# Half of the rounds' modulation columns as weighted rows on VectorE, in a fused fp32 two-block network

## The reference, cut to what matters

```python
c_act = jax.nn.silu(c)                       # (1, 1024)
for layer in range(DEPTH):
    mod = c_act @ mod_w[layer] + mod_b[layer]            # 6 x 1024 columns
    sh1, sc1, g1, sh2, sc2, g2 = jnp.split(mod, N_MOD, axis=-1)
    u = modulate(rms_norm(h, norm_mix[layer]), sh1, sc1)
    mix = hgrn2_mixer(u, ...)                            # layer 0
    h = h + g1[:, None, :] * mix
    u = modulate(rms_norm(h, norm_ffn[layer]), sh2, sc2)
    h = h + g2[:, None, :] * swiglu(u, ffn_w_in[layer], ffn_w_out[layer])
```

## Time and profile before

| | us |
|---|---|
| median of 3 runs | 1589.38 |
| their range | 1589.01 to 1591.5 |
| the profiled execution's own time | 1587.78 |
| its span in the profile | 1585.7 |

### The profile page before, as it was taken

One profiled execution on the slowest core, in us unless ns is written; L12 is line 12 of the kernel. 1 busy time (PEld: TensorE's weight loads), 2 busy tenths in 40 slices (PEclk: granted clock), 3 DMA queues, 4 the chain that ended last, 5 costly groups with the idle time before them and its releaser, 6 DMA issues.

```text
span 1585.7 us, 26563 instructions
## 1 busy us (share of the span) xinstructions
PE 1505.1 (95%) x11356; PEld 1247.4 (79%) x11356; DVE 743.4 (47%) x1185; ACT 581.7 (37%) x899; POOL 28.0 (2%) x47
## 2 busy tenths in 40 slices
PE   7999998999998979999999899989899999999996
PEld 4988898999998649999999768979666656566553
DVE  4658667677767335545555635644221212222121
ACT  3522243444444445444446625542121222212121
POOL 0100000000000001000000000001000000000000
PEclk9999999999989799999999779999999999999998
DMA  9778447978868404555534313716599999999995
GB/s 365 248 237 286 143 135 282 328 269 298 298 222 298 130 1 142 197 186 184 181 114 133 129 37 101 292 54 240 229 418 424 422 420 424 422 420 425 420 420 222
DMA packets 168467, 404.15 MB, mean 255 GB/s; under 512 B 5013, under 2 KB 131250, under 8 KB 155058
## 3 DMA queue, kind: packets, MB, share of 16 engines
q1 hardware_dynamic: 166336, 397.43, 67.4%
q0 software_dynamic: 1648, 5.18, 1.1%
q10 hardware_dynamic: 386, 0.11, 0.0%
HBM read 401.63 MB, written 1.07 MB: 254 GB/s over the span
## 4 chain that ended last, share of the span: by engine, by line
PE 79%; DMA 10%; DVE 7%; ACT 3%; issue 1%; SPq 1%; DVEq 0%; ACTq 0%
PE ps L1797 27%; PE ps L2332 11%; PE ps L2045 7%; PE ps L2354 5%; DMA arena<-in_w 4%; PE ps L1832 4%; PE ps L1810 3%; PE ps L2319 3%; DMA late<-in_w 2%; PE ps L2077 2%; PE ps L1977 2%; PE ps L1906 2%; PE ps L1896 2%; PE ps L2365 1%; DMA arena<-in_mod_w 1%
## 5 line engine op out<-in xcount | busy, mean ns | idle before, releaser
L1797 PE MATMUL ps<-u,wsplit 128*128 128x256 f32 x3912 | 485.9, 285 | 8.5 <-DVE wsplit L1147 6.9
L1797 PEld LDWEIGHTS ps<-u,wsplit 128*128 128x128 f32 x3912 | 477.0, 193 | 16.5 <-DVE wsplit L1147 8.7
L1147 DVE TENSOR_TENSOR wsplit<-arena,wsplit 128x1024 fp32r<-128x1024 f32 x258 | 312.1, 1222 | 255.6 <-ACT wsplit L759 253.9
L759 ACT ACTIVATE wsplit<-arena 128x1024 fp32r<-128x1024 f32 x258 | 270.7, 1056 | 334.2 <-PE ps L1797 161.5
L2332 PE MATMUL ps<-arena 128*64 128x256 f32 x1408 | 156.9, 380 | 4.8 <-DMA arena<-in_w 4.0
L2332 PEld LDWEIGHTS ps<-arena 128*64 128x64 f32 x1408 | 101.2, 137 | 65.9 <-issue 13.6
L2045 PE MATMUL ps<-hid,wsplit 128*128 128x256 f32 x1056 | 130.2, 283 | 0.3 <-DVE hid L1387 0.3
L2045 PEld LDWEIGHTS ps<-hid,wsplit 128*128 128x128 f32 x1056 | 128.2, 192 | 0.5 <-DVE hid L1387 0.5
L1703 DVE TENSOR_TENSOR arena<-arena,ps 128x256 f32<-128x256 f32 x32 | 13.5, 422 | 244.0 <-ACT arena L1106 244.0
L1111 ACT ACTIVATE arena<-ps 64x512 f32<-64x512 f32 x64 | 37.9, 592 | 145.3 <-PE ps L2354 144.5
L1832 PE MATMUL ps<-wsplit,u 128*128 128x256 f32 x672 | 84.9, 288 | 0.0
(11 more groups left out here) (352 smaller groups left out, 1441.1 us busy)
## 6 DMA issues: line engine op xcount, KB each, us to landing
arena<-in_w SPq DMA_DIRECT2D x66, 2048.0 KB, 25.1
late<-in_w SPq DMA_DIRECT2D x30, 2048.0 KB, 25.6
arena<-in_mod_w SPq DMA_DIRECT2D x48, 1024.0 KB, 6.5
arena<-in_ffn_w_in SPq DMA_DIRECT2D x44, 1024.0 KB, 5.3
arena<-in_ffn_w_out SPq DMA_DIRECT2D x22, 1024.0 KB, 5.0
arena<-in_a_w_in SPq DMA_DIRECT2D x16, 1024.0 KB, 8.6
arena<-in_kv_mod_w SPq DMA_DIRECT2D x8, 1024.0 KB, 4.9
arena<-in_kv_w SPq DMA_DIRECT2D x8, 1024.0 KB, 8.2
```

The source lines that it names most:

```text
L759: act.activation(piece_buf(p, 0), piece_src(p), ACT.Copy).then_inc(hi_done, 1)
L1147: dve.tensor_tensor(piece_buf(p, 1), piece_src(p), piece_buf(p, 0).bitcast(F32), ALU.subtract).then_inc(lo_done, 1)
L1797: mm = pe.matmul(o, w_[:, k, :], u[:, x_, k, :], start=first, stop=last)
```

## The change

The 4096 columns 2048 to 6144 of the first modulation matrix are divided. The first 2048 of them (g1, sh2) now go as weighted rows on VectorE: eight new slots of 128 x 2048 weights. The other 2048 (sc2, g2) stay `gemv`, one slot to a round in place of two. The eight rows slots stand in the ring behind the gate and query pairs 2 to 7 (six of them) and behind the value pairs of rounds 0 and 1. VectorE adds the first six up behind gate pieces 3, 5 and 7 and query pieces 1, 3 and 5, and the last two behind `products(1)` and `products(2)`, in the passes r = 0 and r = 1. `row_sums` stands behind the products of round 3, ScalarE copies its result behind the copy of value pair 3, and `columns` stands ahead of round 4's products, where `column(0)` stood. The sum takes the place of the output gates' buffer, which is written only later.

```diff
@@ rows_slot, plan()
-        s = slot("rows", "modkv" if n == 0 else "mod1", 2048 * max(n - 1, 0))
+        s = slot("rows", *(("mod0", 2048), ("modkv", 0), ("mod1", 0), ("mod1", 2048), ("mod1", 4096))[n])
...
-    linear("zf", "a_in", D + 256, 3, "act")
-    linear("q", "a_in", 0, 4, "act")
+    jobs["rows_a"] = []
+    for i in range(1, 8):
+        job, first = (("zf", D), ("q", -D))[i // 4]
+        linear(job, "a_in", first + 256 * i, 1, "act")
+        if i > 1:
+            jobs["rows_a"].append(rows_slot())
     for r in range(8):
         part, first = ("v", 2 * D) if r < 4 else ("g", 3 * D)
         linear(part + str(r), "a_in", first + 256 * (r % 4), 1, "act")
-        gemv(f"gemv_round{r}", "mod0", 2)
-        for k, s in enumerate(jobs[f"gemv_round{r}"]):
-            s["at"] = 2048 + 256 * (2 * r + k)
+        if r < 2:
+            jobs["rows_a"].append(rows_slot())
+        gemv(f"gemv_round{r}", "mod0", 1)
+        jobs[f"gemv_round{r}"][0]["at"] = 4 * D + 256 * r
@@ ScalarE
-                if r % 4 == 3:
-                    gemv_rows(r // 4)
+                if r == 3:
+                    act.wait_ge(rows_mm, 1)
+                    act.activation(gsb[:].rearrange("p a n -> p (a n)"), ps[:, 6, :], ACT.Copy).then_inc(rows_sb, 1)
+                elif r == 7:
+                    gemv_rows(0)
@@ VectorE
+                if n in (3, 5, 7):
+                    weighted_rows(jobs["rows_a"][n // 2 - 1])
...
-            for p in jobs["q"]:
+            for n, p in enumerate(jobs["q"]):
                 lo_upto(p["w"] + LOOKAHEAD)
+                if n in (1, 3, 5):
+                    weighted_rows(jobs["rows_a"][3 + n // 2])
...
                     decayed(r + 1)
                     if r + 1 < 7:
                         products(r + 1)
+                    if r < 2:
+                        weighted_rows(jobs["rows_a"][6 + r])
@@ TensorE
                 if r == 4:
-                    pe.wait_ge(mod_done, 1)
-                    pe.wait_ge(folded, 1)
-                    column(0)
-                gemv(jobs[f"gemv_round{r}"][0:1])
+                    columns(gsb[:].rearrange("p a n -> p (a n)"), 2, modps[:, 16:32]).then_inc(gemv_col, 1)
                 if r < 4:
                     linear_tokens(pair)
+                    gemv(jobs[f"gemv_round{r}"])
                 else:
                     linear(pair[0])
-                gemv(jobs[f"gemv_round{r}"][1:2])
-                if r >= 4:
+                    gemv(jobs[f"gemv_round{r}"])
                     linear(pair[1])
+                if r == 3:
+                    row_sums(0, ps[:, 6, :]).then_inc(rows_mm, 1)
                 round_(r)
-            column(1).then_inc(gemv_col, 1)
+            pe.wait_ge(folded, 1)
+            column(0).then_inc(gemv_col, 1)
```

More of the change, by code:

```diff
@@ L297, in two_blocks @@
         key_sq = late[:, RING * SLOT:].rearrange("p (c t) -> p c t", c=DC)
-        rows_sum = (part(8192, 2048), part(10240, 2048), part(13312, 2048),
+        rows_sum = (part(14336, 2048), part(8192, 2048), part(10240, 2048), part(13312, 2048),
                     late[:, RING * SLOT:])
@@ L901, in ffn_act @@
                     if layer == 0 and i in (4, 8):
-                        act.wait_ge(rows_mm, i // 4)
+                        act.wait_ge(rows_mm, 1 + i // 4)
                         act.activation(gsb[:].rearrange("p a n -> p (a n)"), ps[:, 7, :], ACT.Copy)\
@@ L980, in memory @@
                     drained[0] += 1
-            act.wait_ge(rows_mm, 3)
+            act.wait_ge(rows_mm, 4)
             act.activation(late_rows, ps[:, 4:6, :], ACT.Copy).then_inc(rows_sb, 1)
@@ L1355, in _ @@
                                       ALU.subtract).then_inc(a_lo, 1)
-            dve.wait_ge(gemv_col, 2)
+            dve.wait_ge(gemv_col, 3)
             dve.tensor_tensor(mod[:, 16:48], modps[:, 16:48], vec1[:, 16:48], ALU.add).then_inc(mod_done, 1)
@@ L1400, in new_gains @@
             def new_gains():
-                dve.wait_ge(gemv_col, 4)
+                dve.wait_ge(gemv_col, 5)
                 dve.tensor_tensor(mod[:, 48:80], modps[:, 48:80], vec1[:, 48:80], ALU.add).then_inc(mod_done, 1)
@@ L1417, in last_gains @@
             def last_gains():
-                dve.wait_ge(gemv_col, 5)
+                dve.wait_ge(gemv_col, 6)
                 dve.tensor_tensor(mod[:, 80:112], ps[:, 0, 0:32], vec1[:, 80:112], ALU.add).then_inc(mod_done, 1)
@@ L1840, in column @@
                 pe.wait_ge(gemv_sb, group + 1)
-                first = 16 * (group + 1)
+                first = 16 * (group + 2)
                 for m in range(2):
@@ L2053, in ffn_pe @@
                     if layer == 0 and i in (3, 7):
-                        row_sums(i // 4, ps[:, 7, :]).then_inc(rows_mm, 1)
+                        row_sums(1 + i // 4, ps[:, 7, :]).then_inc(rows_mm, 1)
                     elif layer == 0 and i in (4, 8):
                         pe.wait_ge(mod_done, 3)
-                        columns(gsb[:].rearrange("p a n -> p (a n)"), 1 + i // 4,
+                        columns(gsb[:].rearrange("p a n -> p (a n)"), 2 + i // 4,
                                 modps[:, 32 + 4 * i:48 + 4 * i]).then_inc(gemv_col, 1)
@@ L2146, in _ @@
             pe.wait_ge(x_tc, 2)
-            row_sums(2, ps[:, 4, :])
-            row_sums(3, ps[:, 5, :]).then_inc(rows_mm, 1)
+            row_sums(3, ps[:, 4, :])
+            row_sums(4, ps[:, 5, :]).then_inc(rows_mm, 1)
             def memory(i):
@@ L2166, in late_columns @@
                 if i == 2:
-                    columns(late_rows[:, 0, :], 4, ps[:, 0, 0:16])
-                    columns(late_rows[:, 1, :], 4, ps[:, 0, 16:32]).then_inc(gemv_col, 1)
+                    columns(late_rows[:, 0, :], 5, ps[:, 0, 0:16])
+                    columns(late_rows[:, 1, :], 5, ps[:, 0, 16:32]).then_inc(gemv_col, 1)
             attention_pe("B", lambda i, k: half(kB, i), lambda i, k: half(qB, i),
```

## The result

The changed kernel takes 1599.86 us, the median of 20 runs (1590.64 to 1607.45). The kernel before takes 1586.09 us, again the median of 20 runs (1572.6 to 1595.28); the three runs of 1589 to 1591.5 us shown ahead of the prediction are among them. The medians differ by 13.8 us. The ratio of the runs is 1.0099, with a 95% interval of 1.0077 to 1.0122: 15.7 us slower by the ratio, 12.2 to 19.4 by its interval. The prediction said 1608.7 us, in a range of 1602 to 1616.

What follows compares the result with a forecast made beforehand. TensorE was taken to bound the kernel's rounds, with VectorE close behind. Waits of +13.9 us (round 2) and +11.0 (round 3) less 5.6 saved gave +19.3 on 1589.38, so 1608.7 us, range 1602 to 1616.

Steps and rivals of the forecast that it cites:

- What TensorE saves: Over the rounds, eight `gemv` of 1.00 us go, `row_sums` and `columns` are added; 5.6 us saved outside rounds 2 and 3.
- Gate and query pieces: Six row steps, 13.0 us, fit VectorE's 12.0 us of idle time there and 1.1 before round 0; cost nothing.
- The row step in pass r = 0: Round 2 waits for v3, queued behind the slot this step frees: 25.6 us in place of 11.7, +13.9.
- t: The end of round 1, from which the prediction counts the times of round 2.
- The row step in pass r = 1: Round 3 waits for g4, whose slot this step frees: 22.7 us in place of 11.7, +11.0.
- The clock term: Products of rounds 2 and 3 run on at half clock after idle time: 2.7 us each, bounds nothing and 3.84.
- Landing: Late transfers in rounds 2 and 3: first of two lands 5.2 to 6.1 us after issue, second 7.8 to 8.7.
- Rival 1: Gate and query pieces become VectorE's, a late slot pushing everything behind: +3 us, 1611.7; chance 0.15.
- rival 4: Only the first wait counts, g4's buffer being free sooner, so round 3 has none: 1597.8 us; chance 0.04.
- Rival 2: Transfers stay hidden in rounds 2 and 3, only VectorE's 2.35 us count: -2.1 us, 1587.3; chance 0.04.
- Rival 3: TensorE alone decides, both waits in rounds 2 and 3 vanish: -6.5 us, 1582.9; chance 0.02.
- The sum: Whole kernel: 13.9 + 11.0 - 5.6 = +19.3 us, put on the median of 1589.38: 1608.7 us.

Runs made afterwards that it cites:

- e1: Changed kernel with the two late rows slots behind v2 and v3 in the ring, VectorE's order kept: 1582.19 us, ratio to before 0.9983.
- e4: Changed kernel with the two late row steps working on 64 of 2048 columns, same place and slots: 1601.82 us, ratio to before 1.0093.
- e10: Changed kernel, unedited, third profile: one run, 1591.81 us.
- e5: Changed kernel with v3 ahead of round 2's `gemv` slot in the ring: 1603.28 us, ratio to before 1.0116.
- e8: Changed kernel once more, unedited: 1607.27 us, ratio to before 1.0129.
- e3: Changed kernel with only the first late row step moved ahead of `decayed(1)` in pass r = 0: 1585.91 us, ratio to before 1.0015.
- e7: Changed kernel with both late rows slots behind v2 and v3 and both row steps ahead of `decayed(1)`: 1579.31 us, ratio to before 0.9957.
- e2: Changed kernel with both late row steps ahead of `decayed(1)` in pass r = 0, ring kept: 1579.50 us, ratio to before 0.9948.
- e6: Changed kernel with 12, 9 and 14 matmuls filling TensorE's gaps in rounds 2 and 3: 1600.06 us, ratio to before 1.0076.

## Why the prediction was right, and where it was wrong

**What TensorE saves: right, a little more than forecast.** The rounds without a wait take 10.65 to 10.67 us, and round 1 10.51 (10.7 forecast), round 4 11.42 against 12.05, a gain of 0.63 (0.6 forecast).

**Gate and query pieces: right.** VectorE's 12 us of idle time there are 0.2 now, and PE has no gap. Round 0's products begin at 90.32 us, against 91.32, which is the `gemv` saved; but over the other profiles this start scatters by more than that 1.0.

**The row step in pass r = 0: right.** SyncE's issues came at t + 7.2 (forecast 7.3), the products at t + 18.55 (19.1), with 2.84 us of clock (2.7). Round 2 took 25.23 us where 25.6 were forecast. e1 and e4 show that the queue and not VectorE's 2.35 us made it.

**The row step in pass r = 1: right, its clock too large.** The products began 15.8 us after the end of round 2 (16.2). The clock term was 1.89 us, not 2.7, so the round took 21.52 us and not 22.7. I had taken the price behind 3.75 us of idle time for both. Over the stages seen here it isn't proportional to the gap: 1.60 us behind 2.35 (e1), 2.84 behind 6.72 and 4.15 with a `gemv` between, 1.89 behind 7.50. Nor is it fixed for a gap: behind 7.36 to 7.50 us, in five profiles, it was 1.76 to 2.82 us (e10 and e5). The Trainium skill (TensorE: Matmul & The Clock Gate, Terms) prices throttled time at half of it, and by it a whole round throttled would lose 3.84. The trace agrees with the price: the granted clock reads 0.50 for some 6.0 us from the start of round 2's products and for some 4.0 from the start of round 3's, and half of that is 3.0 and 2.0 us, for 2.84 and 1.89 measured. A round whose products lost 3.84 is in none of the profiles; the most is 2.92 (e8).

**Landing: right by the rows.** v3 took 7.8 us from issue to landing, as in the earlier trace rows, g4 5.5, between the earlier trace rows. The Trainium skill (DMA: Bandwidth & Descriptors, Measured) has 6.15 us for 1 MB, measured on transfers that GpSimd issued. Here, issued by SyncE, the first of a line took 5.2 and 5.5 us from issue to landing, and 5.2 and 6.1 before, so the rows and not that figure fit.

**The rivals.** Rival 1 fell (no gap in the pieces), rival 4 fell (both waits were there, and e3 shows them to be independent). Rival 2, the transfers hidden and only the row step's time counting, is e1: forecast 2.1 us faster, of which 1.1 lie in the stage, measured 0.96 us faster at the stage (86.14 - 85.18), and 3.0 in the medians of the runs made side by side (0.9983, not told from no change). Its mechanism holds, but that the size fits is in part luck: it lacked 1.6 us of clock in round 2, counted 1.1 us of `row_sums` in round 3 that hide in the wait, and gave the other rounds 0.4 too little. Rival 3, TensorE alone, is e7. The measured 1599.86 us lie nearer to rival 4's 1597.8 than to the forecast, so the time alone would have spoken for the wrong mechanism.

**The sum.** The 19.3 us forecast hold round 0's 1.0, which lies ahead of the stage. So 20.3 compare with the stage's 18.35, and 19.3 with the 17.35 by which the end of round 7 moved (194.81 against 177.46): 1.95 too much. Of this 1.2 are round 3 (0.8 the second clock term, 0.4 the start of its products), 0.4 round 2, and 0.4 what rounds 1 and 4 to 7 took less than forecast.

**The step that failed is the last one: "against the median of 1589.38 ... 1608.7".** The sum was put on a base of three runs, and everything behind the rounds was taken to hold still. The forecast stands 8.8 us above the result. Of these 3.3 are the base: over 20 runs the kernel before takes 1586.09. On that base the same sum is 1605.4 and the same range 1598.7 to 1612.7, which holds the measured 1599.86; so this error alone decides it. 1.95 are the sum's size. The other 3.6 (17.35 - 13.8) stay open. The rest of the span scatters by 14.4 us (1394.3 to 1408.7) between executions of the one changed kernel, which is more than enough for it; and by the ratio in place of the medians (15.7 us) only 1.7 are left. Whether the rest is truly shorter in the changed kernel is open too: its three profiles have a mean of 1401.7 us, the two of before 1402.8. Nor is the result itself sure to a few us: the six runs of e8 have a median of 1607.27, inside the forecast's range, and a ratio of 1.0129. The 17.35 us are a ratio of 1.0109, inside both intervals; the sum's 19.3 are 1.0122, at the edge of the first. The range took in the bounds of the waits and of the clock at the two gaps, but had no term for the scatter of a clock elsewhere or for the error of a median of three.

## What to carry to other kernels

Where one queue issues all transfers in order into a ring, a slot is only as free as the step that uses it last: before a step is moved later, read which slot follows it by the ring's length and what stands behind that in the queue. The cure can be the slot's place (e1) or the step's (e2), but it has to free every late transfer of the line (e5). And a sum of waits of one stage foretells the stage; for the whole kernel's time the base needs as many runs as the answer, and the range a term for what the rest scatters.

## What the runs showed of the hardware that I had not expected

The same program's attention stage, with nothing changed near it, ran at a granted clock of 1.00 in one execution and 0.64 and 0.59 in another, and the rest of the span followed from 1394.3 to 1408.7 us. In the trace of the kernel before, where this stage begins some 16 us earlier, the windows 525 to 545 and 545 to 565 stand at 0.75 and 0.82, so the changed kernel can look partly repaid there by chance.

Idle time of only 2.35 us came with 1.60 us of clock behind it (e1), and a wait of 1.20 us for a small copy with 1.5 us in the 24 matmuls behind it (4.61 us in e6 against 3.11 in e1; in e6 three waits of 0.48 to 1.29 us stand in the 25 us before it). In both cases the granted clock still read 1.00 when the work began again, and fell to 0.50 some 1 us later. And 0.80 to 1.50 us of waiting in e1, e2 and e6 left the products at 3.81 us. The size of a gap alone doesn't tell the clock behind it.
